# Expert rows gathered by one indirect DMA of 8 KB rows, or by two of 4 KB rows, in a streaming-encoder layer

## What is computed

```python
def peer(x, wq, keys1, keys2, u_tab, v_tab):        # per token, 8 heads, 16 experts each
    q = (xb @ wq).reshape(PEER_BLOCK, PEER_HEADS, 2, D_KEY_HALF)
    s1 = einsum('thd,hnd->thn', q[:, :, 0], keys1)
    s2 = einsum('thd,hnd->thn', q[:, :, 1], keys2)
    v1, i1 = top_k(s1, 16);  v2, i2 = top_k(s2, 16)
    cand = v1[..., :, None] + v2[..., None, :]      # 16 x 16 sums
    cidx = i1[..., :, None] * N_KEYS + i2[..., None, :]
    top_s, sel = top_k(cand, 16)
    eidx = take_along_axis(cidx, sel)               # 128 experts of 16384
    gate = softmax(top_s)
    act = gelu(einsum('td,thkd->thk', xb, u_tab[eidx]))
    return einsum('thk,thkd->td', gate * act, v_tab[eidx])
```

## Time and profile before

| | |
|---|---|
| time, median of 2 runs | 3630.26 us (3628.14 to 3632.38) |
| profiled execution, its span | 3631.9 us |
| first gather issued, last one issued | 562.2 us, 3606.3 us |
| busy: PE, DVE, POOL, ACT | 2971.6, 2250.8, 1257.1, 379.8 us |
| bytes moved by DMA | 1224.21 MB, of which 1107.36 MB by the gathers |

### The profile page before, as it was taken

The page is one execution under the profiler, slowest core; times in us unless marked ns, Lnnn a source line. Parts: engine busy times, 40 slices in busy tenths (PEclk is TensorE's granted clock), DMA queues, the critical chain, the costliest instruction groups (busy, mean ns, idle before and its releaser), DMA issues.

```text
span 3631.9 us, 32789 instructions
## 1 busy us (share of the span) xinstructions
PE 2971.6 (82%) x9384; PEld 1535.4 (42%) x9384; DVE 2250.8 (62%) x5355; ACT 379.8 (10%) x935; POOL 1257.1 (35%) x1076
## 2 busy tenths in 40 slices
PE   5799997997789778977897799778977897689866
PEld 4457883452335233623352345324532453234421
DVE  2110144668666866687668766876687668665775
ACT  1000111100110011001100110011001100100010
POOL 0000003434343444334434343444344433344433
PEclk8899999999899989998999899989998999899989
DMA  5511218999999999999999999989999999889978
GB/s 179 228 51 65 94 57 335 406 391 366 368 414 388 354 377 406 387 372 360 415 387 376 356 416 387 377 349 421 381 385 351 421 379 386 338 361 369 399 280 352
DMA packets 195323, 1224.21 MB, mean 337 GB/s; under 512 B 23568, under 2 KB 38864, under 8 KB 56592
## 3 DMA queue, kind: packets, MB, share of 16 engines
q0 software_dynamic: 152064, 1107.36, 76.6%
q1 hardware_dynamic: 32304, 103.66, 7.7%
q10 hardware_dynamic: 10752, 10.82, 0.9%
HBM read 1206.09 MB, written 15.67 MB: 336 GB/s over the span
## 4 chain that ended last, share of the span: by engine, by line
PE 50%; DVE 23%; issue 14%; DMA 8%; ACT 3%; POOL 1%; SPq 1%; DVEq 1%; ACTq 0%; POOLq 0%; PEldq 0%
PE expert_sum L726 26%; DVE ring L1005 8%; PE expert_sum L625 7%; PE mm L707 6%; PE expert_sum L631 5%; DMA ring<-in_uv,idx_cur 4%; PE x_ps L670 3%; DMA wq_sb<-in_wq 2%; DVE diag L1016 2%; ACT dots L576 2%; DVE weights L1009 1%; DVE arena L970 1%; DVE arena L963 1%; DVE arena L968 1%; DVE arena L945 1%
## 5 line engine op out<-in xcount | busy, mean ns | idle before, releaser
L726 PE MATMUL expert_sum<-ring,diag 128*128 128x512 f32 (+1 forms) x4224 | 2054.0, 634 | 546.7 <-DVE diag L1016 546.2
L441 POOL DMA_INDIRECT ring<-in_uv,idx_cur x1056 | 1245.3, 1179 | 1770.5 <-PE expert_sum L726 1514.4
L726 PEld LDWEIGHTS expert_sum<-ring,diag 128*128 128x128 f32 (+1 forms) x4224 | 806.4, 199 | 1664.4 <-issue 902.9
L1005 DVE CUSTOM_DVE_ANT_0 ring<-ring,xn_cur 128x1024 f32<-128x1024 f32 x1056 | 1259.8, 1220 | 240.9 <-DMA ring<-in_uv,idx_cur 219.9
L576 ACT ACTIVATE dots<-dots 128x2 f32<-128x2 f32 x528 | 106.9, 202 | 2104.7 <-DVE dots L1005 2104.6
L1009 DVE TENSOR_TENSOR weights<-dots,gate_cur 128x2 f32<-128x2 f32 x528 | 85.2, 161 | 386.7 <-ACT dots L576 385.9
L707 PEld LDWEIGHTS mm<-arena,wq_sb 128*128 128x128 f32 x2304 | 276.8, 192 | 62.1 <-issue 41.8
L707 PE MATMUL mm<-arena,wq_sb 128*128 128x128 f32 (+1 forms) x2304 | 280.8, 275 | 7.1 <-DMA wq_sb<-in_wq 7.0
L1016 DVE TENSOR_TENSOR diag<-ident_sb,weights 128x256 f32<-128x256 f32 x512 | 218.4, 427 | 59.5 <-PE expert_sum L726 2.4
L625 PE MATMUL expert_sum<-ring 128*128 128x256 f32 (+1 forms) x1088 | 240.7, 380 | 2.0 <-DMA ring<-in_w_ret 2.0
L625 PEld LDWEIGHTS expert_sum<-ring 128*128 128x128 f32 (+1 forms) x1088 | 194.0, 181 | 43.3 <-issue 7.6
(11 more groups left out here) (126 smaller groups left out, 1260.4 us busy)
## 6 DMA issues: line engine op xcount, KB each, us to landing
wq_sb<-in_wq SPq DMA_DIRECT2D x80, 512.0 KB, 10.4
ring<-in_uv,idx_cur POOLq DMA_INDIRECT x1056
ring<-in_w_ret SPq DMA_DIRECT2D x12, 1024.0 KB, 5.0
ring<-in_w_conv SPq DMA_DIRECT2D x18, 512.0 KB, 3.9
proj_scratch<-xn_cur ACTq DMA_DIRECT2D x64, 128.0 KB, 1.9
arena<-proj_scratch SPq DMA_DIRECT2D x8, 1024.0 KB
arena<-in_w_ret SPq DMA_DIRECT2D x4, 1024.0 KB, 7.9
w_out_sb<-in_w_out SPq DMA_DIRECT2D x1, 4096.0 KB, 18.7
```

Of the source, the lines that this page charges most:

```text
L441: pool.indirect_dma_start(ring[:, k % RING, :], None, uv, bass.IndirectOffsetOnAxis(ap=idx_cur[:, k:k + 1], axis=0)).then_inc(landed[k % R ...
L726: ins = pe.matmul(expert_sum[0:n, j * 512:(j + 1) * 512], diag[:, s % 2, i, 0:n], ring[:, k % RING, D + j * 512:D + (j + 1) * 512], start= ...
L1005: dve.tensor_tensor_reduce(u, u, xn_cur[:, :], 1.0, 0.0, ALU.mult, ALU.add, dots[:, k:k + 1]).then_inc(dotted, 1)
```

## The change

Each step issues two indirect DMAs of rows of 4 KB where it issued one of 8 KB. The table is viewed as 32768 rows of 4 KB: row 2e is u of expert e and row 2e + 1 is v. The u half goes into the first half of the slot, with a semaphore `u_landed` for each slot, the v half into the second, with `v_landed`. DVE's dot waits for `u_landed`; PE waits for `v_landed` ahead of each slot's matmuls. POOL makes the two sets of indices by integer multiplications (2e, and 2e + 1) in place of the copy. `weights` becomes another name of `dots`.

```diff
-        idx_cur = sb("idx_cur", [P, STEPS], I32)
+        u_rows = sb("u_rows", [P, STEPS], I32)
+        v_rows = sb("v_rows", [P, STEPS], I32)
...
-        weights = sb("weights", [P, STEPS])
+        weights = dots
...
-        landed = [sem(f"landed{i}") for i in range(RING)]
+        u_landed = [sem(f"u_landed{i}") for i in range(RING)]
+        v_landed = [sem(f"v_landed{i}") for i in range(RING)]
...
+            halves = uv.rearrange("e (s d) -> (e s) d", s=2)
+
             def gathers(base, ks):
                 for k in ks:
                     wait_apart(pool, slot_free, base + k + 1)
-                    pool.indirect_dma_start(ring[:, k % RING, :], None, uv,
-                                            bass.IndirectOffsetOnAxis(ap=idx_cur[:, k:k + 1], axis=0)
-                                            ).then_inc(landed[k % RING], 16)
+                    pool.indirect_dma_start(ring[:, k % RING, 0:D], None, halves,
+                                            bass.IndirectOffsetOnAxis(ap=u_rows[:, k:k + 1], axis=0)
+                                            ).then_inc(u_landed[k % RING], 16)
+                    pool.indirect_dma_start(ring[:, k % RING, D:2 * D], None, halves,
+                                            bass.IndirectOffsetOnAxis(ap=v_rows[:, k:k + 1], axis=0)
+                                            ).then_inc(v_landed[k % RING], 16)
...
-                pool.tensor_copy(idx_cur[:, half], idx_next[:, half]).then_inc(idx_copied, 1)
-                wait_apart(pool, idx_copied, 2 * t + i + 1)
+                pool.tensor_scalar(u_rows[:, half], idx_next[:, half], 2, None, ALU.mult).then_inc(idx_copied, 1)
+                pool.tensor_scalar(v_rows[:, half], idx_next[:, half], 2, 1, ALU.mult, ALU.add).then_inc(idx_copied, 1)
+                wait_apart(pool, idx_copied, 4 * t + 2 * i + 2)
...
                     for i in range(PAIR):
                         k = s * PAIR + i
+                        pe.wait_ge(v_landed[k % RING], t * 16 * (STEPS // RING) + 16 * (k // RING + 1))
...
-                        dve.tensor_copy(idx_cur[rows, 0:steps], idx_next[0:DEC, cols]).then_inc(idx_copied, 1)
+                        dve.tensor_scalar(u_rows[rows, 0:steps], idx_next[0:DEC, cols], 2, None,
+                                          ALU.mult).then_inc(idx_copied, 1)
+                        dve.tensor_scalar(v_rows[rows, 0:steps], idx_next[0:DEC, cols], 2, 1,
+                                          ALU.mult, ALU.add).then_inc(idx_copied, 1)
...
-                        dve.wait_ge(landed[k % RING], t * 16 * (STEPS // RING) + 16 * (k // RING + 1))
+                        dve.wait_ge(u_landed[k % RING], t * 16 * (STEPS // RING) + 16 * (k // RING + 1))
```

More of the change, by code:

```diff
@@ L456, in _ @@
                 gathers(t * STEPS, range(2 * RING, STEPS))
-            pool.wait_ge(idx_copied, 2 * TILES + QUADS)
+            pool.wait_ge(idx_copied, 4 * TILES + 2 * QUADS)
             gathers(TILES * STEPS, range(SAMPLE_STEPS))
@@ L979, in mixer @@
                 settle()
-                wait(dve, idx_copied, 2 * t)
+                wait(dve, idx_copied, 4 * t)
                 dve.scalar_tensor_tensor(idx_next[0:n, :], pick_f[0:n, 0, :], float(NK), pick_f[0:n, 1, :],
```

## The result

The changed kernel takes 3718.54 us (3717.12 to 3719.96, 2 runs) where the kernel before takes 3630.26: ratio 1.025, 95% interval 1.0218 to 1.0281, slower. The forecast was 3754 with a range of 3665 to 3885. The time lies between rival A (3709) and the forecast.

A forecast was written before the change was run, and what follows sets the result against it. The DMA engines, nine tenths busy, were taken to bound the gathers, with POOL becoming later than them after the change. 14.9 us a tile, times 8 is 119, plus 5 for the sample gave 3756, or 3754 us as median; range 3665 to 3885.

The forecast's parts named there:

- rival A: Pure DMA stretches: the DMA engines decide at 2.58 us a step, POOL just keeps up; 3709 us, chance 0.25.
- Packets: DMA queue: 144 more packets a step for the same bytes cost 0.09 us, step 2.49 to 2.58 us.
- POOL's issues: Pure DMA stretches: two issues a step take POOL 2.66 us against 2.49 now; 9.5 us over 56 steps a tile.
- rival B: Pure DMA stretches: dots hold POOL's issues as often as now, 2.96 us a step; about 3900 us, chance 0.14.
- Change of tile: Between tiles: POOL's eight refills become sixteen, the first as early as now; cost 0.
- Mixed stretch: 33 steps a tile at about 3.0 us, where wq loads share the engines: packets alone cost 3.0 us.
- Index work: POOL's second-half index multiplications, between the 16th and 17th gather, cost 1.0 us a tile.
- DVE's stretch: End of a tile, 32 steps: DVE goes on deciding, half the steps pay for packets, 1.4 us a tile.
- v's wait: PE before each slot's matmuls: v lands about 1.3 us after u and is covered; v-gather waits under 50 us.
- Pure DMA: Stretches 1320 to 1420 and 1520 to 1560 us, about 56 steps a tile, bounded by DMA at 2.49 us a step.
- C: Packets are cheap where something else is late too, so only pure DMA stretches pay: 3675 us, chance 0.15.
- D: Ring's round trip is the limit, so u's earlier landing makes it faster: 3487 or likelier 3560 us, chance 0.04.

The follow-up runs named there:

- x5: Changed kernel with DVE's dot replaced by a plain sum of u and POOL's slot wait two steps stricter (at most 12 gathers outstanding): 3665.64 us, ratio 1.0092.
- x9: Changed kernel whose second gather fetches 2 KB of each v row instead of 4 KB: 3881.3 us, ratio 1.0682.
- x8: Changed kernel with POOL's wait for a free slot two steps stricter, at most 12 gathers outstanding: 3808.65 us, ratio 1.0483.
- x7: Kernel before with POOL's wait for a free slot four steps stricter, at most 4 gathers of 8 KB rows outstanding: 4789.28 us, ratio 1.3202.
- x10: Kernel before with one gather of 6 KB instead of 8 KB per row: 3568.49 us, ratio 0.9825.
- x4: Changed kernel with DVE's dot waiting for the v half as well as the u half: 3959.68 us, ratio 1.0893.
- x11: Changed kernel with DVE's dot waiting for u and v, and POOL's slot wait two steps stricter (at most 12 gathers outstanding): 3957.6 us, ratio 1.0885.
- x1: Kernel before with DVE's dot product replaced by a plain sum of the u half, one SBUF input: 3609.89 us, ratio 0.993.
- x2: Changed kernel with DVE's dot product replaced by a plain sum of the u half: 3886.51 us, ratio 1.0687.

## Why the prediction was right, point by point

**Packets.** 304128 in the software queue, as forecast; the share rose by 2.1 points (forecast about 2). That is 78.7% of 3717.9 us against 76.6% of 3631.9, 144 us more on each DMA engine or 0.14 us a step where I had 0.09; in x5 it is 0.10. x5's stretch shows 0.12 for packets and bare issues together. The term was of the right size.

**POOL's issues.** Right in kind: POOL passed the DMA engines in the stretch 24 to 56, and x5 and x9 show it. The term 2.66 us a step, from the bursts, was too low: it measured 2.82 (90.4 / 32), and the mean issue 1.12 us where 1.03 was my sign and 1.18 rival B's. "Mostly clear of the next" is the step that failed: a late POOL keeps meeting dots. Of its issues 46% start within a dot, and 49% did before. And the stretch was shorter: I charged 56 steps a tile, 32 paid.

**Change of tile.** "The first is as early as now, 0" was wrong. The first starts 16.3 to 18.0 us before the restart, where it was 18.3 to 20.5; the sixteenth is not early at all. 16 issues at 1.3 us outlast the change of tile. But what DVE waits for is not a row of the burst: the mixer's load of `conv_scratch` meets the burst, and DVE waits 5.3 us longer for it in each tile. I had looked at the first gather, and at gathers only. That the burst delays the load fits x5 and x8, where the burst pauses before the restart and the wait is gone; no run changed the load itself.

**Mixed stretch.** Forecast +3, measured -4.1 a tile, 25 us over six tiles, and the cause is open. wq lands in 7.3 us instead of 10.4, but that goes with the kind of chip: it is 9.6 to 10.4 in all traces of the second kind, one or two gathers a step, and 7.1 to 7.8 in all of the first, the kernel before with a ring of 4 (x7) among them. And the waits for wq that are gone are small: 7.0 us of PE's matmuls in the whole run, 19.7 of its weight loads, partly the same time. x10 has 0 and 3.6 of them and still takes 120.5 us for this stretch.

**Index work, DVE's stretch, v's wait.** PE's matmuls name no wait for a v gather and its weight loads one of 0.4 us, as said; the index multiplications took 0.55 and 0.41 us on average, together the 1.0. The DVE stretch gave +0.2 for 1.4. Of DVE's longer wait for u, 438 us, most is in steps 24 to 56 (27.9 us a tile against 11.9): there it is POOL's lateness seen from DVE.

**The reading of what bounds.** "Pure DMA" was too strong for steps 24 to 48, as x10 shows, and right for the sample. It happened not to matter, because the new bound was POOL. The sample's +5.1 us (forecast 5.4) fits.

**Sum.** Forecast 119 + 5.4. Measured 6 x 11.3 + 9.7 (tile 0) + 5.9 (the last) + 5.1 (sample) - 2.7 (an earlier start) = 86, the spans' difference. Per tile I was 5.2 us too low in steps 24 to 56 and 4.0 too low in steps 0 to 8, and too high by 7.1 in the mixed stretch, 2.8 in steps 8 to 24, 1.2 in DVE's stretch and 1.7 in the rest. That leaves 14.9 against 11.3: the mechanism was right in kind, but that the total came so near is partly luck. The rows also hang together: while DVE waits in steps 0 to 8, POOL issues ahead, and that may be why steps 8 to 24 lose nothing; in x8, where the cap forbids it, they lose 7.2 us.

Rival A (3709) came nearer by number, but its mechanism, POOL just keeping up, is what the trace excludes. B had the right mechanism for the issue's length and too many steps. C is out, as POOL decides. D is out as a whole, since the kernel is slower; whether u's early landing pays back a part was asked by x4 and x11 only, and the late handovers cover it.

## What to carry to other kernels

Splitting a gather doubles what the issuing engine does, so add up that engine's issues with their gaps and holds over the densest stretch, and over each burst: the last issue counts, not the first, and so do other engines' loads that fall into it. A DMA share of 1.0 does not prove that DMA decides. Taking a quarter of the bytes away tells it, stretch by stretch (x10: no shorter in steps 24 to 48, 24% shorter in the sample), and reading the GB/s beside the share shows an engine that carries less. Before explaining a difference between two batches by the edits, see whether they ran on the same chip, and put the unedited kernel into every batch.

## What was new about the hardware

- An indirect DMA's issue is held by a DVE instruction with two SBUF inputs and not by one with one: mean 1179 ns against 968 (x1), 1117 and 1125 against 987 and 977 (x5), and 0.94 us within L1036, which has one SBUF and one PSUM input and writes as much as the dot. That is the Trainium skill's rule, page "SBUF — State Buffer", section "Who interferes with whom", now with the counter-test.
- Gathers of 4 KB rows at a DMA share of 1.01 moved 398 GB/s (x5) where 8 KB rows moved 418 (the kernel before, steps 24 to 48).
- On two of four chips, five kernels with two indirect DMAs per step (the unedited changed kernel not among them) had handovers between engines up to 13 us late and took 3881 to 3972 us. What delays them is open. It comes with at most 12 gathers outstanding (x11), with a quarter fewer bytes (x9) and with no hold by the dots (x2).
